# Differential attention written out through its 32 tiles, with the heads' loads asked for ahead of most late conditioning pieces

## The reference

```python
def diff_attention(q, k, v, lam, g_sub, lam_init):
    b, nq = q.shape[:2]
    nb = nq // Q_BLOCK
    qb = q.reshape((b, nb, Q_BLOCK) + q.shape[2:]).swapaxes(0, 1)
    scale = DA_QK_DIM ** -0.5

    def one(qblk):
        s = jnp.einsum('bqhsd,bkhsd->bhsqk', qblk, k).astype(jnp.float32) * scale
        p = jax.nn.softmax(s, axis=-1)
        a = p[:, :, 0] - lam * p[:, :, 1]
        return jnp.einsum('bhqk,bkhe->bqhe', a.astype(v.dtype), v)

    o = lax.map(one, qb).swapaxes(0, 1).reshape(b, nq, DA_HEADS, DA_V_DIM)
    o = rms_norm(o, g_sub) * (1 - lam_init)
    return o.reshape(b, nq, DA_HEADS * DA_V_DIM)
```

## Time and profile before

| | us |
|---|---|
| median of 3 runs | 1982.87 |
| lowest, highest | 1979.5, 1984.51 |
| the profiled execution, its time | 1977.57 |
| its span, first to last instruction | 1975.5 |
| busy in the span: PE, DVE, POOL, ACT | 1818.9, 1110.9, 829.2, 763.1 |
| from the first scores of `diff` (582.3) to ACT's last work in it (813.0) | 230.7 |

### The profile page before, as it was taken

The page is one execution under the profiler, slowest core; times in us unless marked ns, Lnnn a source line. Parts: engine busy times, 40 slices in busy tenths (PEclk is TensorE's granted clock), DMA queues, the critical chain, the costliest instruction groups (busy, mean ns, idle before and its releaser), DMA issues. The chain is left out here.

```text
span 1975.5 us, 26948 instructions
## 1 busy us (share of the span) xinstructions
PE 1818.9 (92%) x9312; PEld 1534.5 (78%) x9312; DVE 1110.9 (56%) x1559; ACT 763.1 (39%) x1434; POOL 829.2 (42%) x516
## 2 busy tenths in 40 slices
PE   6897999999979989697999989789999999899998
PEld 4896888887758768496988868668888888688886
DVE  2336588778838878375763345485545444322322
ACT  2424333434327667453540025543333333232332
POOL 0124667776416994200001212375555555233433
PEclk9898999999989999898989999899999999999999
DMA  7233323435575555203012342112122221354552
GB/s 271 85 104 108 129 107 146 152 128 213 192 191 145 131 142 153 91 2 77 0 65 96 144 174 86 69 70 96 64 96 76 83 96 64 114 195 143 197 175 90
DMA packets 84201, 235.18 MB, mean 119 GB/s; under 512 B 11025, under 2 KB 24721, under 8 KB 83986
## 3 DMA queue, kind: packets, MB, share of 16 engines
q1 hardware_dynamic: 84114, 234.09, 35.9%
HBM read 180.19 MB, written 53.87 MB: 118 GB/s over the span
## 5 line engine op out<-in xcount | busy, mean ns | idle before, releaser
L677 POOL TENSOR_TENSOR ring<-raw_w,ring 128x512 fp32r<-128x512 f32 x120 | 181.1, 1521 | 162.9 <-ACT ring L566 162.7
L78 PE MATMUL psum<-h_hi,ring 128*128 128x512 f32 x400 | 156.3, 391 | 8.4 <-ACT z L612 4.2
L79 PE MATMUL psum<-h_lo,ring 128*128 128x512 f32 x400 | 155.7, 389 | 0.0
L80 PE MATMUL psum<-h_hi,ring 128*128 128x512 f32 x400 | 155.6, 389 | 0.0
L2473 DVE TENSOR_TENSOR u_lo<-stage,u_hi 128x1024 fp32r<-128x1024 f32 x44 | 58.5, 1331 | 160.7 <-ACT u_hi L2433 160.7
L78 PE MATMUL psum<-u_hi,uf_hi 128*128 128x512 f32 x352 | 138.2, 393 | 9.7 <-POOL uf_lo L2456 9.4
L2456 POOL TENSOR_TENSOR uf_lo<-u_f,uf_hi 128x512 fp32r<-128x512 f32 x44 | 78.2, 1778 | 158.9 <-ACT uf_hi L2435 158.6
L79 PE MATMUL psum<-u_lo,uf_hi 128*128 128x512 f32 x352 | 137.9, 392 | 0.0
L80 PE MATMUL psum<-u_hi,uf_lo 128*128 128x512 f32 x352 | 137.9, 392 | 0.0
L566 ACT ACTIVATE ring<-raw_w 128x512 fp32r<-128x512 f32 x120 | 73.7, 626 | 136.1 <-DVE raw_w L802 58.1
L1224 DVE TENSOR_REDUCE mx<-psum 128x1 f32<-128x1280 f32 x64 | 95.2, 1487 | 24.4 <-PE psum L1121 22.2
(11 more groups left out here) (323 smaller groups left out, 5098.4 us busy)
## 6 DMA issues: line engine op xcount, KB each, us to landing
stage<-in_w_ffn_out SPq DMA_DIRECT2D x44, 512.0 KB, 3.6
raw_w<-in_w_pairs SPq DMA_DIRECT2D x40, 512.0 KB, 4.6
qk_dram<-room SPq DMA_DIRECT2D x26, 512.0 KB, 3.6
room<-in_w_ada SPq DMA_DIRECT2D x24, 512.0 KB, 5.6
gates_dram<-ost SPq DMA_DIRECT2D x24, 512.0 KB, 3.0
b_g<-gates_dram SPq DMA_DIRECT2D x8, 1536.0 KB, 7.9
stage<-in_w_ff SPq DMA_DIRECT2D x22, 512.0 KB, 4.8
i_raw<-in_w_ff SPq DMA_DIRECT2D x22, 512.0 KB, 4.7
```

The source lines that it names most:

```text
L78: pe.matmul(out, sh, mh, start=first, stop=False, skip_group_check=onto)
L79: pe.matmul(out, sh, ml, start=False, stop=False, skip_group_check=onto)
L80: return pe.matmul(out, sl, mh, start=False, stop=last, skip_group_check=onto)
L677: pool.tensor_tensor(w_lo[i], source(p, i), w_hi[i].bitcast(F32), ALU.subtract).then_inc(w_lo_ready, 1)
```

## The change

`TILES` becomes 32 (`DA_HEADS * TL`) and the loop over `it` is gone on PE, ACT and DVE: one pipeline of 35 steps, every step written out. All semaphore counts and all addresses become constants. Head buffers are chosen by `h % 2`, values by `t // TL % 2`. SP's list is put in another order. No arithmetic changes.

```diff
-    TILES = 2 * TL
+    TILES = DA_HEADS * TL
...
-        USES = (3 * TILES + 2) // 2
-
-        def slot(it, i, what):
+        def slot(i, what):
 
             n = 3 * (i - LAG_TURN) + RING.index(what)
-            return n % 2, it * USES + n // 2
+            return n % 2, n // 2
...
             sp.wait_ge(av_done, TL)
             load_head(io, sp, 2, heads[0], head_in[0])
-            for n in range(RING_P, 12):
+            for j in range(2):
+                sp.dma_start(keep["stage"][j][:], io["late"][:, j * D:(j + 1) * D]).then_inc(stage_in, 16)
+            for n in range(RING_P, 6):
                 load_piece(n)
             sp.wait_ge(av_done, 2 * TL)
             load_head(io, sp, 3, heads[1], head_in[1])
+            for n in range(6, 12):
+                load_piece(n)
+            sp.wait_ge(av_done, TL * 3)
+            load_window_qk(io, sp, 0, window_buffers(keep), keep["qk_in"])
             for n in range(12, PIECES):
                 load_piece(n)
-            for j in range(2):
-                sp.dma_start(keep["stage"][j][:], io["late"][:, j * D:(j + 1) * D]).then_inc(stage_in, 16)
-            sp.wait_ge(av_done, TL * 3)
-            load_window_qk(io, sp, 0, window_buffers(keep), keep["qk_in"])
             sp.wait_ge(stage_in, 32)
...
-            with pe.Fori(0, 2) as it:
-                for i in range(STEPS):
-                    t = i - LAG_TURN
-                    if i < TILES:
-                        scores(it, i)
...
+            for i in range(STEPS):
+                t = i - LAG_TURN
+                if i < TILES:
+                    scores(i)
...
                 if t >= 1:
-                    act.activation(o[:, bass.ds(it * TILES + (t - 1), 1), :].rearrange("p a n -> p (a n)"),
+                    act.activation(o[:, t - 1:t, :].rearrange("p a n -> p (a n)"),
                                    banks[6 + b][:, 2 * P:3 * P], ACT.Copy, scale=rec[:, (t - 1) % 4, 0:1]).then_inc(o_ready, 1)
```

More of the change, by code:

```diff
@@ L1105, in _, with use, scores @@
         def _(pe):
-            def use(it, i, what):
-                b, used = slot(it, i, what)
+            def use(i, what):
+                b, used = slot(i, what)
                 pe.wait_ge(free[b], used + 1)
                 return b, banks[6 + b]
-            def scores(it, i):
-                j, t = i // TL, i % TL
+            def scores(i):
+                h, t = divmod(i, TL)
+                j = h % 2
                 if t == 0:
-                    pe.wait_ge(head_in[j], 16 * HEAD_DMAS * it + 16 * HEAD_DMAS)
+                    pe.wait_ge(head_in[j], 16 * HEAD_DMAS * (h // 2 + 1))
                 for s in range(2):
-                    pe.wait_ge(exp_done[s], it * TILES + i + 1)
+                    pe.wait_ge(exp_done[s], i + 1)
                     q = q_st[j][:, s, t * P:(t + 1) * P]
@@ L1122, in scores, with turn @@
                     mm.then_inc(sc_done[s], 1)
-            def turn(it, t, i, what):
-                b, bank = use(it, i, what)
+            def turn(t, i, what):
+                b, bank = use(i, what)
                 for n, k in enumerate(KEYS[what]):
@@ L1132, in products @@
                 for k in range(TT):
-                    mm = pe.matmul(bank[:, 2 * P:3 * P], at[t % 2][:, k, :], val[t // TL][:, k, :], start=(k == 0), stop=(k == TT - 1))
+                    mm = pe.matmul(bank[:, 2 * P:3 * P], at[t % 2][:, k, :], val[t // TL % 2][:, k, :], start=(k == 0), stop=(k == TT - 1))
                 return mm
-            with pe.Fori(0, 2) as it:
-                for i in range(STEPS):
-                    t = i - LAG_TURN
-                    if i < TILES:
-                        scores(it, i)
[L1141 to L1157, removed]
-                        for what in ("low", "high"):
-                            b, mm = turn(it, t, i, what)
-                            mm.then_inc(turned[b], 1)
-                pe.sem_inc(turned[slot(it, STEPS - 1, "low")[0]], 1)
@@ new lines, in _ @@
+            for i in range(STEPS):
+                t = i - LAG_TURN
+                if i < TILES:
+                    scores(i)
+                if t >= 0:
+                    if t < TILES:
+                        pe.wait_ge(a_ready, t + 3)
+                        b, mm = turn(t, i, "last")
+                    else:
+                        b, bank = use(i, "last")
+                    if t >= 1:
+                        for what in ("low", "high"):
+                            bb, used = slot(i - 1, what)
+                            pe.wait_ge(free[bb], used + 2)
+                        mm = products(t - 1, banks[6 + b])
+                        mm.then_inc(av_done, 1)
+                        pe.wait_ge(av_done, t)
+                        pe.sem_inc(turned[b], 1)
+                    else:
+                        mm.then_inc(turned[b], 1)
+                if 0 <= t < TILES:
+                    for what in ("low", "high"):
+                        b, mm = turn(t, i, what)
+                        mm.then_inc(turned[b], 1)
@@ L1163, in _, with exp @@
         @block.scalar
         def _(act):
-            def exp(it, i, s):
-                N = it * TILES + i
+            def exp(i, s):
+                N = i
                 act.wait_ge(neg_ready[s], N + 1)
@@ L1171, in exp, with copy_out @@
                                bias=neg_m[:, i % 2, s:s + 1], accum_out=sums[:, i % 2, s:s + 1]).then_inc(exp_done[s], 1)
-            def copy_out(it, i, what):
-                b, used = slot(it, i, what)
+            def copy_out(i, what):
+                b, used = slot(i, what)
                 act.wait_ge(turned[b], used + 1)
@@ L1178, in copy_out, with copy_last @@
                                banks[6 + b].rearrange("p (k n) -> p k n", n=P), ACT.Copy).then_inc(free[b], 1)
-            def copy_last(it, i):
-                b, used = slot(it, i, "last")
+            def copy_last(i):
+                b, used = slot(i, "last")
                 t = i - LAG_TURN
@@ L1204, in _, with maximum, reciprocals @@
                 act.sem_inc(exp_done[s], 1)
[L1205 to L1218, removed]
+            for i in range(STEPS):
+                if i < TILES:
+                    exp(i, 0)
+                if i >= LAG_TURN:
+                    copy_last(i)
+                if i < TILES:
+                    exp(i, 1)
+                if LAG_TURN <= i < TILES + LAG_TURN:
+                    copy_out(i, "low")
+                    copy_out(i, "high")
+                if i >= LAG_AV:
+                    square(i - LAG_AV)
         @block.vector
         def _(v):
-            def maximum(ch, it, i, s):
-                v.wait_ge(sc_done[s], it * TILES + i + 1)
+            def maximum(ch, i, s):
+                v.wait_ge(sc_done[s], i + 1)
                 ch.link(v.tensor_reduce(mx[:, s:s + 1], psum[:, 3 * s * HALF:3 * s * HALF + TOK], AX.X, ALU.max))
                 v.tensor_scalar(neg_m[:, i % 2, s:s + 1], mx[:, s:s + 1], -SCALE, None, ALU.mult).then_inc(neg_ready[s], 1)
-            def reciprocals(ch, it, i):
+            def reciprocals(ch, i):
                 for s in range(2):
-                    v.wait_ge(exp_done[s], it * TILES + i + 2)
+                    v.wait_ge(exp_done[s], i + 2)
                 ch.link(v.reciprocal(rec[:, i % 4, :], sums[:, i % 2, :]))
@@ L1233, in reciprocals, with combine @@
                                         ALU.mult, ALU.mult))
-            def combine(it, t):
+            def combine(t):
                 if t >= 2:
-                    b, used = slot(it, t - 2 + LAG_TURN, "high")
+                    b, used = slot(t - 2 + LAG_TURN, "high")
                     v.wait_ge(turned[b], used + 1)
@@ L1244, in _ @@
             v.sem_inc(a_ready, 2)
[L1245 to L1256, removed]
+            ch = Chain(v, dve)
+            for i in range(STEPS):
+                if i < TILES:
+                    maximum(ch, i, 0)
+                    maximum(ch, i, 1)
+                if 1 <= i < TILES + 1:
+                    combine(i - 1)
+                if i < TILES:
+                    reciprocals(ch, i)
 def window(nc, sem, banks, io, keep):
```

13 lines of the change are left out of this document (6 added, 7 removed).

## The result

| | before | after |
|---|---|---|
| median, us | 1983.49 (4 runs) | 1961.38 (4 runs) |
| lowest, highest | 1979.5, 1984.51 | 1959.12, 1961.81 |
| the profiled execution, its time | 1977.57 | 1961.0 |
| its span | 1975.5 | 1959.2 |

The ratio, worked out over the runs, is 0.9898, with the 95% interval 0.9884 to 0.9913; the quotient of the two medians is 0.9889. Ratios further on are of the first kind. The change is faster by 22.1 us in the medians and by 16.6 us between the two profiled executions; 15.6 us and a median of 1967.3 were forecast. So the kernel became faster as the prediction had it. But the median lies 1.6 us under the forecast's own range (1963 to 1972) and only 0.4 us inside the wide one (1961 to 1974), whose low end came from the scatter of runs and from no mechanism.

What follows compares the result with a forecast made beforehand. `diff` was taken as bound by PE inside a turn and by a drained pipeline at the seam; 12.7 (seam) + 2.9 (registers) = 15.6 us, so 1962.0 profiled, median 1967.3, own range 1963 to 1972, wide range 1961 to 1974.

Steps and rivals of the forecast that it cites:

- The seam: Between tiles 15 and 19 in `diff`: no emptying and refilling of the pipeline, gain 12.7 us, low end 10.8.
- The rival reading: At the turn's branch: the hole is an instruction fetch stall, worth 2.4 us; no chance given.
- Registers: ACT's L1186 in the chain PE waits for: constants save 0.10 us a step over 29 steps, 2.9 us.
- The upper bound: PE's whole wait for ACT's bank vanishes, 0.38 us a step, 11 us in all, giving 1959; chance 0.05.
- Head 3 and SP's order: Head 3 requested at 701.1, landed 726, wanted 734.2: cost nothing; the old order would hand back 13 us.
- Pieces: POOL's late pieces wait behind head 3 and the window's load, ending between 795 and 798: cost nothing.
- The cover at the end: At `diff`'s end: POOL finishes 1 to 4 us ahead of ACT; rival that POOL ends last, 1973, chance 0.10.
- my two ways: Piece 12's start on POOL: 773 (window landed, plus some 3 us) or 776.5 (24.6 us, as behind a head).
- Instructions: Rival in the second half: written-out PE stands for instructions beside two loads, 40 us, giving 2007; chance 0.04.
- The step that was off: Last step of the sum: profiled forecast 1962.0 plus 5.3 us to the median gives 1967.3.

Runs made afterwards that it cites:

- its second run: The kernel before, unchanged, timed and traced again as a control: median 1982.61 us, ratio 0.9997.
- ACT's loop: The change, but ACT alone runs steps 3 to 26 as two turns of twelve, with registers: median 1961.94 us, ratio 0.9898 to the kernel before.
- each half alone: The change with SP's old order: 1982.76 us, ratio 1.0005; the looped kernel before with SP's new order: 1983.45 us, ratio 1.0008.
- POOL lighter: POOL's pooling work and late-piece products in `diff` left out, in the kernel before (1982.11 us, ratio 0.9999) and in the change (1963.5 us, 0.9898).

## Why the prediction was right, and where it was off

*The seam.* 12.7 us forecast; 38.12 - 25.04 = 13.1 in the two traces, of which 0.4 are the four steps' registers. The reading of the earlier trace rows, that the hole is the order of the work and not the branch, is shown: without a branch and with the drain it was still 36.88 and 37.10 us. The rival reading, a stall of 2.4 us at the branch, was wrong about the hole but right that there is one, and the table load of 1.28 beside it was not in my sum. Stall, table and four steps' registers together were worth 1.2 us with SP's old order (38.12 to 36.88), and since 15 to 19 was counted whole, they were in the 12.7.

The clock was in it too, and I gave it no term. The same 25 us, from 698 to 723, in the traces of the kernel before, of its second run, of the loop with SP's new order and of the change (the last figures but two are the granted clock):

```profile
698.00:723.00 25.00, 18.08 (x96) 14.99 (x97) 19.85 (x28) 15.38 (x26) 23.82 (x21) 0.93 0.32 100
698.00:723.00 25.00, 16.71 (x77) 13.66 (x76) 16.01 (x21) 12.49 (x22) 23.82 (x21) 0.86 0.35 111
698.00:723.00 25.00, 16.80 (x73) 13.68 (x74) 16.33 (x23) 11.85 (x19) 6.75 (x8) 0.80 1.02 234
698.00:723.00 25.00, 24.21 (x170) 21.24 (x170) 22.22 (x29) 18.54 (x41) 11.32 (x9) 1.00 0.94 202
```

The clock fell to 1.2 GHz for a part of this stretch wherever PE had paused at the seam, and never in the change. The seams took 38.12, 40.06, 42.23 and 25.04 us: the lower the clock, the longer. An estimate from the rows, 25 us times the missing share, gives 1.8, 3.5 and 5.0 us, so most of what separates the three looped seams; in the third, ACT's longer stand (5.56 us) is mixed in. In both kernels that were written out with the drain kept it is 0.93 too, so the 12.1 us of the drain hold some 1.8 of lower clock.

*Registers.* 0.10 us a step forecast; 6.353 - 6.26 = 0.09 here, and 0.10 switched on and off by ACT's loop. The upper bound, the whole wait of 0.38, did not come: 0.29 stayed, and it took another order on PE to get it, worth 0.24 a step.

*Head 3 and SP's order.* Asked for at 699.01 (701.1 forecast), and no step waited. That the order earns nothing by itself and lets the seam's gain through is shown from both sides: each half alone gives a ratio of 1.0005 and 1.0008. The amount that the old order hands back was forecast 5 us too small: 13 against 18.3, of which 1.85 are the clock after the wait.

*Pieces.* Piece 6 started at 723.87 (725.7), pieces 6 to 11 were done at 758.1 (758.7), the window's load was released at 749.05 (751.9), piece 12 started at 770.16 (773 to 776.5), POOL ended at 791.87 (795 to 798) and ACT at 798.18 (797.4). POOL stood 14.1 and 12.0 us where I had some 20 and then 14 to 18, as piece 5 ended at 709.8 and not 705.3. The cover at the end was 6.3 us, not 1 to 4. The mis-sized part is the release of the window's load: with steps of 6.26 ahead of it and behind the seam it came 2.9 us earlier, and I had moved POOL's end by 2 only, in a side remark. From release to piece 12 it took 21.1 us, the low one of my two ways (18.4 and 3), and the last four pieces took 21.7 (21.8).

*Instructions.* q8 brought blocks in the second half too, as said:

```profile
q8 instruction: 5, 0.08, 0.4%
```

(700 to 797 us after the change; the second half had none before.) No step beside head 3's load, 700 to 725 us, is over 6.26. Which engine the blocks belong to isn't shown, but bringing them cost PE nothing that can be seen.

**The step that was off** is the last of the sum, "That execution lies 5.3 us under the median of the runs, 1982.87, so the median should be 1967.3". The forecast for the profiled execution was 1962.0, and it took 1961.0. The step takes for granted that the changed kernel's profiled execution would lie as far under its median. But the changed kernel's profiled execution lay 0.4 us under its median, not 5.3. The trace of before was a low one: of the 75 timed runs of that kernel three were faster than its 1977.57, and later traces of the looped form have spans of 1981.6, 1979.0 (SP's new order) and 1979.6 (POOL lighter) against its 1975.5. Where the spans differ can be told in part. The looped form's `diff` takes 229.2, 231.7 and 231.2 us from its first score to its last product, the change's 214.7, 214.3, 215.3 and (POOL lighter) 214.6: 14.5 to 17.4 us less; the refill at the seam is one part that varies (38.12, 40.06, 38.30). Code outside `diff` is the same in all of them, yet over all the traces the time ahead of its first score scatters from 580 to 586 us and that behind its last product from 1161 to 1165.5, in both forms alike. The medians of the four comparisons differ by 22.1, 19.1, 19.8 and 18.6 us. By the middles of both, 20 against 16, some 4 us more than `diff` shows remain. Some 0.6 of them lie outside the span: a run of the kernel before took 1.8 to 4.9 us more than its span, 2.4 in the mean, and every run of the change 1.7 to 1.8. The rest is left open: POOL's work does not account for it, and no run tried the stages outside `diff`. That the median fell inside the wide range is luck to that extent: the mechanisms gave 1967, and an excess that nobody forecast nearly carried it out.

## What to carry to other kernels

Where a software pipeline has to be a loop, don't let the turn's end be the pipeline's end: the drain and refill cost 12 us at the seam, the branch with its table load under 1 us with little traffic, some 4.7 beside a head's load (with the lower clock in it), and nothing where the pipeline stayed full. A pipeline that runs on makes every load behind the seam due earlier, so reckon the queue's order again in the same edit; either half alone was worth nothing here. And ask of each short wait that stands in every step whether work without need of it can stand there instead: that was worth some 6 us more in the traces (5 and 10 in the medians), for moving a few lines.

## What the runs showed of the hardware that I had not expected

- ACT stood 2.37 us at a turn's start with little traffic, 5.56 us beside a head's load (one trace), and nothing to be seen where the pipeline stayed full.
- Where PE paused at the seam or for a head, the granted clock fell to 1.2 GHz and stayed there into the work that followed: 1.85 us more for tile 24's scores after 16.2 us of waiting, and 0.93 to 0.80 in the mean over a looped seam's 25 us. The pipeline that runs on kept 2.4 GHz.
- A turn of the loop on ACT loaded the exponential's table again, 1.28 us, where the first exponential stood inside the loop, and not where it stood ahead of it.
- Registers on ACT, a 51 ns instruction in a chain from PE over ACT back to PE, cost 0.10 us a step, twice that instruction's length, switched on for 24 steps and off for those behind them in one run.
- DVE's combine took 1.54 us alone and up to 3.7 beside POOL's two-input operations.
